# Making the two output tiles of a weight block together: a hybrid attention, state-space and feed-forward layer

## The reference, cut to what matters

```python
u = rmsnorm(h, mix_pre_norm[l])
proj = u @ w_in[l]
q, k, v, z, xbc, dt_raw, g_a, g_b = _split(proj, IN_WIDTHS)
y_attn = banded_sink_attention(rope(q), rope(k), v, attn_sinks[l]) @ w_attn_out[l]
y_ssd = ssd_mixer(z, xbc, dt_raw, ...) @ w_ssd_out[l]      # xbc: causal conv of 4 taps, then SiLU
merged = sigmoid(g_a) * y_attn + sigmoid(g_b) * y_ssd
h = h + rmsnorm(merged @ w_out[l], mix_post_norm[l])
f = rmsnorm(h, ffn_pre_norm[l]) @ w_up[l]                  # width 2 * 2816
f_gate, f_val = _split(causal_dwconv(f, ffn_conv_w[l], ffn_conv_b[l]), (D_FF, D_FF))
h = h + rmsnorm((silu(f_gate) * f_val) @ w_down[l], ffn_post_norm[l])
```

## Time and profile before

| | |
|---|---|
| runs (3) | 1127.31, 1129.58, 1131.26 us; median 1129.58 us |
| span of the profiled execution | 1130.6 us |
| PE busy | 1100.1 us, 97% of the span, 5409 matmuls |
| PE weight load busy | 914.0 us, 81% (beside PE) |
| DVE busy | 656.0 us, 58% |
| ACT busy | 448.7 us, 40% |
| POOL busy | 131.9 us, 12% |
| share of the chain that ended last | PE 90%, DVE 3%, ACT 2%, issue 2% |

### The profile page before, as it was taken

How to read it: one execution, slowest core, us unless ns; L and a number is a source line. 1 busy time by engine, 2 the same in 40 slices (tenths; PEclk the granted TensorE clock), 3 DMA queues, 4 the chain that set the end, 5 groups by cost and what they waited for, 6 DMA issues and landing times.

```text
span 1130.6 us, 14815 instructions
## 1 busy us (share of the span) xinstructions
PE 1100.1 (97%) x5409; PEld 914.0 (81%) x5409; DVE 656.0 (58%) x943; ACT 448.7 (40%) x688; POOL 131.9 (12%) x197
## 2 busy tenths in 40 slices
PE   6999999998999999999999999989999999999997
PEld 6887888778877987788888888879888888888886
DVE  6885668573876686684343222366666666662214
ACT  5464346333463455453232213255344343431212
POOL 7012201320022102210000000220000000000001
PEclk9998999898989999899999999999999999999999
DMA  7230132012310322023224234442133242333221
GB/s 202 87 95 1 39 112 78 18 37 78 96 37 1 111 76 76 1 75 112 74 77 129 93 111 149 149 112 76 42 106 104 82 111 78 108 108 109 82 75 75
DMA packets 111608, 95.53 MB, mean 84 GB/s; under 512 B 15343, under 2 KB 101691, under 8 KB 111547
## 3 DMA queue, kind: packets, MB, share of 16 engines
q1 hardware_dynamic: 111547, 94.74, 27.7%
HBM read 92.63 MB, written 2.10 MB: 84 GB/s over the span
## 4 chain that ended last, share of the span: by engine, by line
PE 90%; DVE 3%; ACT 2%; issue 2%; DMA 1%; POOL 1%; SPq 0%; DVEq 0%; POOLq 0%; ACTq 0%
PE ps L1165 17%; PE ps L1166 17%; PE ps L1167 17%; PE ps L1172 10%; PE ps L1173 9%; PE ps L1174 9%; PE ps L1386 2%; PE ps L1331 2%; PE ps L1408 1%; PE ps L1333 1%; DVE wlo L764 1%; PE ps L1398 1%; PE ps L1382 1%; PE ps L1207 1%; PE ps L1307 1%
## 5 line engine op out<-in xcount | busy, mean ns | idle before, releaser
L764 DVE TENSOR_TENSOR wlo<-raw,whi 128x2048 fp32r<-128x2048 f32 (+1 forms) x83 | 189.1, 2280 | 224.5 <-ACT whi L433 224.5
L1165 PE MATMUL ps<-uhi,whi 128*128 128x512 f32 x640 | 249.2, 389 | 0.0
L1167 PE MATMUL ps<-uhi,wlo 128*128 128x512 f32 x640 | 249.1, 389 | 0.0
L1166 PE MATMUL ps<-ulo,whi 128*128 128x512 f32 x640 | 249.0, 389 | 0.0
L433 ACT ACTIVATE whi<-raw 128x2048 fp32r<-128x2048 f32 (+1 forms) x83 | 156.2, 1883 | 178.6 <-PE ps L1174 98.1
L1172 PE MATMUL ps<-whi,uhi 128*128 128x512 f32 (+1 forms) x320 | 129.3, 404 | 11.7 <-issue 5.9
L1167 PEld LDWEIGHTS ps<-uhi,wlo 128*128 128x128 f32 x640 | 120.2, 188 | 25.2
L1165 PEld LDWEIGHTS ps<-uhi,whi 128*128 128x128 f32 x640 | 120.1, 188 | 25.1 <-DVE wlo L764 0.2
L1166 PEld LDWEIGHTS ps<-ulo,whi 128*128 128x128 f32 x640 | 120.2, 188 | 24.4
L1173 PE MATMUL ps<-whi,ulo 128*128 128x512 f32 (+1 forms) x320 | 125.1, 391 | 0.0
L1174 PE MATMUL ps<-wlo,uhi 128*128 128x512 f32 (+1 forms) x320 | 124.9, 390 | 0.0
(11 more groups left out here) (222 smaller groups left out, 1490.9 us busy)
## 6 DMA issues: line engine op xcount, KB each, us to landing
raw<-in_w_in_dram SPq DMA_DIRECT2D x24, 1024.0 KB
raw<-in_w_up_dram SPq DMA_DIRECT2D x44, 512.0 KB
raw<-in_w_down_dram SPq DMA_DIRECT2D x11, 1024.0 KB
raw<-in_w_in_dram SPq DMA_DIRECT2D x16, 512.0 KB
raw<-in_w_ssd_out_dram SPq DMA_DIRECT2D x8, 1024.0 KB
raw<-in_w_attn_out_dram SPq DMA_DIRECT2D x4, 1024.0 KB
raw<-in_w_out_dram SPq DMA_DIRECT2D x4, 1024.0 KB
yT<-in_x_dram SPq DMA_DIRECT2D x4, 512.0 KB, 5.2
```

What stands on the lines that cost most here:

```text
L764: dve.tensor_tensor(wlo[sl][:, 0:width] if into is None else into, raw[sl][:, 0:width], h.bitcast(F32), ALU.subtract).then_inc(s["lo_done" ...
L1165: pe.matmul(bank(b)[:, span], hi_[:, k, c], ah[:, span], start=first and k == 0, stop=False)
L1166: pe.matmul(bank(b)[:, span], hi_[:, k, c], al[:, span], start=False, stop=False)
L1167: ins = pe.matmul(bank(b)[:, span], lo_[:, k, c], ah[:, span], start=False, stop=last and k == KD - 1)
```

## The change

A new function `feature_pair` makes the two tiles of a block in one pass over the 8 slices. In each slice six products follow one another, and each goes to the other bank than the one before: hi*hi of the even tile, hi*hi of the odd, hi*lo of the even, hi*lo of the odd, lo*hi of the even, lo*hi of the odd. It returns the last matmul of either tile, and these carry the same semaphores as before. All calls of `features` are replaced but those of the first two blocks of the up stage. Since both banks are written from the first slice on, the waits for the banks stand together ahead of the pair in `conv_tiles`.

```diff
--- before.py
+++ after.py
@@ -1167,6 +1167,22 @@
                     ins = pe.matmul(bank(b)[:, span], lo_[:, k, c], ah[:, span], start=False, stop=last and k == KD - 1)
                 return ins
 
+            def feature_pair(b, sl, acts, first=True, last=True, span=slice(0, S), split=None):
+
+                hi_, lo_ = (tiles(w, KD) for w in split or (whi[sl][:, :], wlo[sl][:, :]))
+                f0, f1 = slice(0, P), slice(P, 2 * P)
+                o0, o1 = bank(b)[:, span], bank(b + 1)[:, span]
+                for k in range(KD):
+                    ah, al = acts(k)
+                    begin, end = first and k == 0, last and k == KD - 1
+                    pe.matmul(o0, hi_[:, k, f0], ah[:, span], start=begin, stop=False)
+                    pe.matmul(o1, hi_[:, k, f1], ah[:, span], start=begin, stop=False)
+                    pe.matmul(o0, hi_[:, k, f0], al[:, span], start=False, stop=False)
+                    pe.matmul(o1, hi_[:, k, f1], al[:, span], start=False, stop=False)
+                    even = pe.matmul(o0, lo_[:, k, f0], ah[:, span], start=False, stop=end)
+                    odd = pe.matmul(o1, lo_[:, k, f1], ah[:, span], start=False, stop=end)
+                return even, odd
+
             def tokens(o, ah, al, wh, wl, first, last):
 
                 pe.matmul(o, ah, wh, start=first, stop=False)
@@ -1243,17 +1259,16 @@
 
                 def conv_tiles(j):
                     sl = block_ready(j)
-                    for m in range(2):
-                        f = 2 * (j - 2) + m
-                        if f == 0:
-                            pe.wait_ge(s["o_sb"], G * NT)
-                        elif f == 1:
-                            pe.wait_ge(s["y_done"], G * NT)
-                        elif f == 3:
-                            pe.wait_ge(s["yT_sb"], G * NT + 1)
-                        elif f >= 4:
-                            pe.wait_ge(s["conv_ok"], G * 6 + (f - 3))
-                        features(4 + f % 4, sl, m, u).then_inc(s["conv_mm"] if m == 0 else s["blk_done"], 1)
+                    if j == 2:
+                        pe.wait_ge(s["o_sb"], G * NT)
+                        pe.wait_ge(s["y_done"], G * NT)
+                    elif j == 3:
+                        pe.wait_ge(s["yT_sb"], G * NT + 1)
+                    else:
+                        pe.wait_ge(s["conv_ok"], G * 6 + 2)
+                    even, odd = feature_pair(4 + 2 * (j % 2), sl, u)
+                    even.then_inc(s["conv_mm"], 1)
+                    odd.then_inc(s["blk_done"], 1)
 
                 conv_tiles(2)
                 conv_tiles(3)
@@ -1421,8 +1436,9 @@
                 n = i * 2 + N_C1
                 pe.wait_ge(s["lo_done"], n + 1)
                 pe.wait_ge(s["ga_tanh"], i * 2)
-                features(0, 0, 0, u).then_inc(s["ga_mm"], 1)
-                features(1, 0, 1, u).then_inc(s["blk_done"], 1)
+                even, odd = feature_pair(0, 0, u)
+                even.then_inc(s["ga_mm"], 1)
+                odd.then_inc(s["blk_done"], 1)
                 if first:
                     pe.wait_ge(s["yn_ok"], NG * NT)
                     pe.wait_ge(s["st_ok"], NG * (NT - 1))
@@ -1435,8 +1451,9 @@
                         pe.wait_ge(s["split_lo"], k + 1)
                     return rhi[:, KD + k, :], rlo[:, KD + k, :]
 
-                features(2, 1, 0, o).then_inc(s["at_mm"], 1)
-                features(3, 1, 1, o).then_inc(s["blk_done"], 1)
+                even, odd = feature_pair(2, 1, o)
+                even.then_inc(s["at_mm"], 1)
+                odd.then_inc(s["blk_done"], 1)
 
             gate_a(0, True)
             with pe.Fori(1, NG) as i:
@@ -1451,18 +1468,20 @@
                     pe.wait_ge(s["lo_done"], i * 6 + (N_C2 + q + 1))
                     if j == 0:
                         pe.wait_ge(s["gb_tanh"], i * 4 + 2 * r)
-                        features(4, q % 2, 0, u).then_inc(s["gb_mm"], 1)
-                        features(5, q % 2, 1, u).then_inc(s["blk_done"], 1)
+                        even, odd = feature_pair(4, q % 2, u)
+                        even.then_inc(s["gb_mm"], 1)
+                        odd.then_inc(s["blk_done"], 1)
                     elif j == 1:
                         pe.wait_ge(s["so_ok"], i * 4 + 2 * r)
                         y = lambda k: (rhi[:, k, :], rlo[:, k, :])
-                        features(6, q % 2, 0, y, True, False)
-                        features(7, q % 2, 1, y, True, False).then_inc(s["blk_done"], 1)
+                        even, odd = feature_pair(6, q % 2, y, True, False)
+                        odd.then_inc(s["blk_done"], 1)
                     else:
                         pe.wait_ge(s["split_lo"], KD + KI)
                         y = lambda k: (rhi[:, KD + k, :], rlo[:, KD + k, :])
-                        features(6, q % 2, 0, y, False, True).then_inc(s["so_mm"], 1)
-                        features(7, q % 2, 1, y, False, True).then_inc(s["blk_done"], 1)
+                        even, odd = feature_pair(6, q % 2, y, False, True)
+                        even.then_inc(s["so_mm"], 1)
+                        odd.then_inc(s["blk_done"], 1)
 
             def all_tokens(n, n0, acts_hi, acts_lo, tile_ok, bank_ok, done, between=lambda t, b: None):
 
@@ -1549,8 +1568,9 @@
                     J = i * 2 + q
                     pe.wait_ge(s["lo_done"], J + (N_E + 1))
                     pe.wait_ge(s["f_ok"], J - 1)
-                    features(2 * q, q, 0, u).then_inc(s["up_mm"], 1)
-                    features(2 * q + 1, q, 1, u).then_inc(s["blk_done"], 1)
+                    even, odd = feature_pair(2 * q, q, u)
+                    even.then_inc(s["up_mm"], 1)
+                    odd.then_inc(s["blk_done"], 1)
 
             with pe.Fori(1, KF // 2) as i:
                 up(i)
```

## The result

| | before | after |
|---|---|---|
| median of the runs (4 each) | 1128.44 us | 1142.31 us |
| lowest and highest | 1126.91, 1131.26 | 1139.67, 1145.17 |
| ratio, 95% interval | | 1.0122 (1.0096 to 1.0149) |
| span of the profiled execution | 1130.6 us | 1137.9 us |

The changed kernel is 1.2% slower, 13.9 us by the medians. The forecast was 1144.0 us, counted from a median of before of 1129.58 us.

The account below looks back on a forecast made before the run. PE is busy 97% of the span, so only matmul pace and new holes matter. Profiled 1130.6 + 12.4 (holes, four groups) + 2.0 (clock) = 1145.0, 1.0 over the runs' median: 1144.0 us, range 1134 to 1152.

Parts of the forecast that it names:

- The pace: All paired stages, 2496 matmuls: changing the bank costs or saves nothing, 0 us; spacing stays 0.227 us.
- rivals of the pace: All paired stages: strict bank alternation saves up to 13.3 ns on each of 2496 matmuls, 1111 us; chance 0.08.
- cycled banks: Dense stages: alternating banks idles PE and drops the clock; a tenth of 2496 matmuls slower is 20 us, 1164; chance 0.03.
- The first hole: Start of conv block 4 in each group: the late even tile delays VectorE's wlo, so PE waits 1.38 us.
- The second hole: Before the second half of z in each group: wlo of block 6 waits for whi, PE starts 1.73 us later.
- The clock: New holes slow 12 matmuls of a z half in half the groups, 2.0 us; rival with more slow stretches, 1150, chance 0.13.
- The upper bound: Most the clock could cost in the groups: two more 24-matmul losses in each, 4 x 2 x 1.0, 8 us.
- The waits: Sign of being right: PE's waits for wlo go from five to nine or more places, 5.8 to about 18 us.
- Up stage, gates, transfers: Later work stays hidden, cost 0: up stage slack 1.8 us, wlo between gates 0.37 later, loads up to 2.4 us later.

Follow-up runs that it names:

- conv_old: Changed kernel, but the groups' conv blocks made one tile after the other with old waits; pairs stay in gates and up stage: 1128.83 us, ratio 1.0005.
- reorder2: Changed kernel, VectorE's wlo and silu 0 ahead of dt chain, tanh 3 and silu 3 ahead of tile 4's taps, ScalarE's whi of blocks 4, 6 earlier: 1133.60 us.
- early_silu: Kernel before, no pairs, with tanh 4 ahead of tap 5 on ScalarE and silu 4 ahead of taps 5 on VectorE: 1126.29 us, ratio 0.9983.
- waits_only: Kernel before, no pairs, but in conv blocks the waits for both banks stand ahead of the even tile: 1127.72 us, ratio 0.9995.
- lead4: Changed kernel, but in the conv blocks the even tile runs 4 slices ahead of the odd one: 1126.66 us, ratio 0.9991.
- pair_b3: Changed kernel, but of a group's three conv blocks only block 3 is made as a pair: 1127.81 us, ratio 0.9998.

## Why the prediction was right

*The pace.* Predicted 0 for 2496 matmuls, and the spacing is 0.2267 us in the changed kernel's up stage as in the old one's (over more than 880 matmuls of each), with the granted clock at 1.00 (870.79 to 881.67). conv_old shows the same by the time. Two changes of bank in the trace of before were enough to tell. The rivals of the pace and of cycled banks are refuted.

*The first hole.* Predicted 1.38 us a group, measured 1.54 at the start of block 4 and 1.68 at its end. The way was as written: tap 0 late, VectorE late, no gap up to `wlo`. The 0.16 at the start is a tap that follows the even tile by 0.1 more than I took, and a PE that starts 0.14 instead of 0.05 after the subtraction. The other 0.14 I had not counted: behind the hole the first matmuls start further apart, so that the block takes 11.01 to 11.03 us instead of 10.88 or 10.89.

*The second hole.* Predicted 1.73, measured 1.86. I had `whi` of block 6 as the last thing in front of `wlo`. In the trace it ends at 77.02 (75.11 + 1.91) and `wlo` starts at 77.35, right behind the masked decays: VectorE's own list was the last. The two estimates were 0.13 us apart (77.66 and 77.79), so the size held, but the releaser I named was the wrong one. Counted from the end of block 4, `whi` was done 0.16 us earlier than I had it, because tanh 5 starts 0.03 us behind taps 5 and not 0.19. VectorE was 0.26 us later than I had it, and that is the sum of two errors: silu 5 beside GpSimd took 1.52 us and not 0.69, and from its end to `wlo` it was 1.52 us and not 1.97. That they cancelled in part was luck. reorder2 moves both `whi` and silu 3, so its 0.5 us alone would not tell the two apart; the rows do.

*The clock.* This term failed: I added 2.0 us for slow stretches that the holes would bring. From the first product with `whi` to the last product of z, about 4 us before gate a, the kernels without holes and the changed one read (stretch; its length; busy us and count of PE, PEld, DVE, ACT, POOL; clock; DMA share; GB/s), first before, then the changed one, then conv_old:

```profile
16.40:489.70 473.30, 462.53 (x2463) 382.80 (x2464) 336.54 (x596) 222.39 (x437) 94.60 (x105) 0.94 0.21 61
```

```profile
15.70:496.60 480.90, 458.70 (x2464) 377.70 (x2465) 336.83 (x596) 220.19 (x437) 93.64 (x107) 0.96 0.21 60
```

```profile
15.60:483.40 467.80, 457.26 (x2464) 378.50 (x2464) 335.98 (x596) 222.19 (x437) 94.50 (x105) 0.96 0.21 61
```

The clock was no lower with the holes. Nor was it in the timed runs: a mean granted clock of 0.980 over the 60 runs of the six kernels with new holes, 0.979 over the 89 of before. The profiled execution of before had a low one, 0.974, as low as the lowest of its timed runs (0.974 to 0.985), which is why the two profiled spans differ by 7.3 us only, of 14.2 us of holes. conv_old, which has the holes of before, is 5.5 us shorter in this stretch than before itself. The sum came near the measured time partly by luck: the two holes were 1.7 us short over four groups and the clock 2.0 us long. What is left of the difference between 1144.0 and 1142.31 is mostly the median from which I counted, 1129.58 and not 1128.44. The upper bound was also wrong: two losses of 24 matmuls in each group are, by the difference of 1.97 us in the earlier trace rows, 16 us and not 8.

*The waits.* Of the signs of being right, one failed in part. PE waits for `wlo` in nine places, as written, but for 9.3 us in all and not 18: in the second hole most of the idle time stands in front of the copies of q and of tile 1 (6.5 us), which come before `wlo` in PE's list.

*Up stage, gates, transfers.* Predicted 0. Slack in the up stage 1.8 us, measured 1.7. From the first product of gate a to the end of the span it is 636.8 us before and 637.2 in the changed kernel. The `wlo` between gate a and gate b ends 0.35 us later against the start of gate a, where I had 0.37. At the rate that I used, 1.9 MB in 10.88 us, a block of 1 MB takes 6.0 us and not 5.5, which changes nothing against the 10 us there are; no run took transfers apart.

## What to carry to other kernels

When two results are finished together instead of one after the other, the work of the second is not late, but that of the first is, by nearly the time of one result; look for what in the followers' lists stands behind it with a deadline, and subtract the slack that exists. Whether a pace depends on which bank comes next can be read from the places where the bank changes already. Of two things that will become ready within 0.2 us of one another, a timeline of before does not tell which will be last; the trace of the changed kernel does.

## What the runs showed that I had not expected

Behind the first hole the first matmuls are slower: the block of 48 took 11.03 us in group 0, 0.14 more than the 10.89 of before. Most of it is between the first two starts, 0.33 us; the next nine distances are 0.224 to 0.236, and the granted clock is 1.00.

```profile
56.63 0.49 PE L1178 MATMUL ps<-uhi,whi 128*128 128x512 f32 x1 [1.40 <-DVE wlo L764]
56.96 0.39 PE L1179 MATMUL ps<-uhi,whi 128*128 128x512 f32 x1
```

It isn't the idle time alone. In the kernel before, gate a starts with no idle time, behind small matmuls, and its first distance is 0.34 us (493.84 to 494.18).

Beside GpSimd's two products (line 366), VectorE's silu and masked decays take longer: in group 0 before, silu 5 took 1.53 us beside them and silu 4, ahead of them, 0.69. The taps, one operand of which is in PSUM, do not: three of them beside another pair of these products took 2.32 us, as elsewhere.

```profile
72.41 2.58 POOL L366 TENSOR_TENSOR seg_lo<-tri,adt_lo 128x512 fp32r<-128x512 f32 x2 [18.96 <-PE ps L1308]
72.56 1.53 DVE L845 SCALAR_TENSOR_TENSOR conv<-tanh_c,conv 128x512 f32<-128x512 f32 x1
...
51.40 2.04 POOL L366 TENSOR_TENSOR seg_lo<-tri,adt_lo 128x512 fp32r<-128x512 f32 x2 [23.20 <-DVE adt_lo L899]
51.15 2.32 DVE L836 SCALAR_TENSOR_TENSOR conv<-ps,cwg,conv 128x511 f32<-128x511 f32 x3
```

 The two silu and the two masked decays together took 3.88 us before and 3.63 in the changed kernel, where silu took more of it and the decays less. In early_silu silu 5 began 0.15 us ahead of GpSimd's first product and took 0.69 us, and the decays took 2.59 us instead of 1.74. Moving VectorE's work by a few tenths moved this loss, and did not save it.

What the clock does from one execution to the next is worth more than most of these effects: five kernels without new holes (before, conv_old, waits_only, lead4, pair_b3) took 464.7 to 473.3 us from the first product to the last of z.
